# Four column strips for the conditioning products and the cached value pages of a two-layer decoder step

## What is computed

```
cmod = silu(c)                              # 1 prompt row, 8 sample rows
mod  = cmod @ ada_w[l] + ada_b[l]           # 6 x 1024 columns for each layer
hm   = rmsnorm(x, g) * (1 + sc1) + sh1      # and so on with sc2, sh2, g1, g2

p = softmax(concat([s_p, s_n]))             # sample rows: 1024 cached keys and the new one
o = einsum(p[..., :P], v_cached) + einsum(p[..., P:], v_new)
```

## Time and profile before

| | |
|---|---|
| median of three runs | 1906.09 us |
| the profiled execution | 1905.32 us, its span 1903.2 us |
| PE busy | 1763.3 us, 93% |
| DVE, ACT, POOL busy | 892.9, 597.2, 198.6 us |
| mean granted clock of TensorE | 0.954 |
| HBM | 224 MB read, 23.7 MB written |

### The profile page before, as it was taken

The page is one execution under the profiler, slowest core; times in us unless marked ns, Lnnn a source line. Parts: engine busy times, 40 slices in busy tenths (PEclk is TensorE's granted clock), DMA queues, the critical chain, the costliest instruction groups (busy, mean ns, idle before and its releaser), DMA issues.

```text
span 1903.2 us, 33709 instructions
## 1 busy us (share of the span) xinstructions
PE 1763.3 (93%) x13817; PEld 1593.5 (84%) x13817; DVE 892.9 (47%) x1470; ACT 597.2 (31%) x880; POOL 198.6 (10%) x172
## 2 busy tenths in 40 slices
PE   5899767889999999999999999999978999999997
PEld 4799744349899999998988878798748899999996
DVE  3328578764533332333625547337464533333334
ACT  2324234343432122122334334314432432122222
POOL 1006560001000000001000201101120100000001
PEclk8799777899999999999999999999988999999998
DMA  8946644556636236327232716334846133333321
GB/s 247 276 124 186 195 138 122 163 142 155 158 97 166 80 98 164 92 74 180 73 94 73 234 50 199 115 89 141 257 151 166 56 89 100 87 95 95 89 69 54
DMA packets 368714, 248.96 MB, mean 131 GB/s; under 512 B 9768, under 2 KB 338888, under 8 KB 368591
## 3 DMA queue, kind: packets, MB, share of 16 engines
q1 hardware_dynamic: 333716, 197.04, 36.8%
q0 software_dynamic: 9296, 33.82, 5.2%
q10 hardware_dynamic: 25587, 16.45, 2.9%
HBM read 224.05 MB, written 23.70 MB: 130 GB/s over the span
## 4 chain that ended last, share of the span: by engine, by line
PE 76%; DVE 11%; ACT 5%; DMA 3%; POOL 2%; issue 2%; SPq 1%; ACTq 0%; POOLq 0%; DVEq 0%
PE product L824 56%; PE product L839 4%; PE job L774 2%; DVE CV L1904 2%; POOL sqa L2364 2%; PE job L1269 2%; PE product L1017 2%; PE job L1252 1%; PE job L1186 1%; PE job L715 1%; DVE SC L1918 1%; DMA raw<-in_ada_w 1%; PE job L978 1%; DVE scaled L1831 1%; PE job L1169 1%
## 5 line engine op out<-in xcount | busy, mean ns | idle before, releaser
L824 PE MATMUL product<-H_hi,w_lo 128*128 128x260 f32 x2368 | 672.4, 284 | 5.0 <-ACT gate L1301 4.7
L824 PE MATMUL product<-H_lo,w_hi 128*128 128x260 f32 x2368 | 670.5, 283 | 0.0
L824 PE MATMUL product<-H_hi,w_hi 128*128 128x260 f32 x2368 | 670.3, 283 | 0.0
L824 PEld LDWEIGHTS product<-H_hi,w_lo 128*128 128x128 f32 x2368 | 447.8, 189 | 6.4 <-DVE w_lo L1775 5.5
L824 PEld LDWEIGHTS product<-H_lo,w_hi 128*128 128x128 f32 x2368 | 447.8, 189 | 1.4
L824 PEld LDWEIGHTS product<-H_hi,w_hi 128*128 128x128 f32 x2368 | 448.1, 189 | 0.0
L1775 DVE TENSOR_TENSOR w_lo<-raw,w_hi 128x1024 fp32r<-128x1024 f32 (+1 forms) x228 | 278.1, 1220 | 207.2 <-ACT w_hi L1301 206.5
L1301 ACT ACTIVATE w_hi<-raw 128x1024 fp32r<-128x1024 f32 (+1 forms) x228 | 234.9, 1037 | 254.9 <-PE product L824 186.8
L824 PE MATMUL product<-G_hi,w_lo 128*128 128x260 f32 x880 | 250.2, 284 | 2.7 <-DVE G_lo L1784 1.4
L824 PE MATMUL product<-G_hi,w_hi 128*128 128x260 f32 x880 | 249.4, 283 | 0.0
L824 PE MATMUL product<-G_lo,w_hi 128*128 128x260 f32 x880 | 249.3, 283 | 0.0
(11 more groups left out here) (329 smaller groups left out, 2232.5 us busy)
## 6 DMA issues: line engine op xcount, KB each, us to landing
spare<-in_ada_w SPq DMA_DIRECT2D x48, 512.0 KB, 7.3
raw<-in_w_in_odd SPq DMA_DIRECT2D x48, 512.0 KB, 3.9
raw<-in_w_ffn_gate SPq DMA_DIRECT2D x44, 512.0 KB, 4.2
raw<-in_w_ffn_up SPq DMA_DIRECT2D x44, 512.0 KB, 3.9
kp<-in_cache_k SPq DMA_DIRECT2D x64, 256.0 KB, 2.9
raw<-in_w_ffn_down SPq DMA_DIRECT2D x32, 512.0 KB, 4.6
st<-in_state_ret POOLq DMA_DIRECT2D x28, 512.0 KB, 4.7
out_ret_sample<-st POOLq DMA_DIRECT2D x28, 512.0 KB, 5.0
```

The source lines that it names most:

```text
L824: mm = pe.matmul(Gp[slot][:, c, 0:CH], w[:, j, k, :], x[:, k, cols], start=k == 0 and p == 0, stop=k == kt - 1 and p == 2)
```

## The change

The products of a contraction tile go to four strips in turn instead of two, each strip takes two of the eight tiles (or pages), and what follows handles four parts:

- conditioning products: strip by `i % 4`, the first four matmuls start their strip, the last four stop it;
- ACT copies 128 partitions instead of 64, and the `rows_` tiles are 128 partitions high;
- the turn is 128 by 128 instead of 64 rows by 128;
- DVE sums four parts with a reduce into `mod` and adds the bias in a second instruction;
- value pages: strip by `g % 4`; masking and gathering go over 104 partitions instead of 40, with the constants that they need repeated four times;
- the memset of the product banks covers 128 partitions.

The order of the work, the loads, the semaphores and the buffers are the same. The diff, without the places where a tile's height alone changes in the same way:

```diff
     at[0] = lg_at
-    vm = sb("vm", [CG + HEADS, 2, 512])
+    vm = sb("vm", [3 * CG + HEADS, 2, 512])
     at[0] = free_at
...
-    rows_early = sb("rows_early", [2 * CG, 2, 512])
+    rows_early = sb("rows_early", [P, 2, 512])
...
 
-            return slice(CG * (i % 2), CG * (i % 2) + CG)
+            return slice(CG * (i % 4), CG * (i % 4) + CG)
...
                             mm = pe.matmul(bank[group_rows(k), j * P:(j + 1) * P], cT[:, k, :], site_buffer(name)[:, b, k, :],
-                                           start=k < 2, stop=k >= KD - 2)
+                                           start=k < 4, stop=k >= KD - 4)
                     close(mm)
...
                 for j in range(4):
-                    mm = turn(bank[:, j * 2 * CG:(j + 1) * 2 * CG], ada_rows(g)[:, j * P:(j + 1) * P], 2 * CG)
+                    mm = turn(bank[:, j * P:(j + 1) * P], ada_rows(g)[:, j * P:(j + 1) * P], P)
                 close(mm)
...
-                    n.up(f(ada_rows(g), Jp[jobs.bank(("adr", g))][0:2 * CG, :], ACT.Copy), emptied["A"])
+                    n.up(f(ada_rows(g), Jp[jobs.bank(("adr", g))][:, :], ACT.Copy), emptied["A"])
...
                     pe.wait_ge(v_page[g], 16 * (b + 1))
-                    mm = pe.matmul(value_bank(b)[CG * (g % 2):CG * (g % 2) + HEADS, :], SC[:, :, b, g],
-                                   value_page(g), start=g < 2, stop=g >= 6)
+                    mm = pe.matmul(value_bank(b)[CG * (g % 4):CG * (g % 4) + HEADS, :], SC[:, :, b, g],
+                                   value_page(g), start=g < 4, stop=g >= 4)
                     mm.then_inc(v_used, 1)
...
                     mm = pe.matmul(Gp[1][:, 1, t * NB + b:t * NB + b + 1], vm[:, b % 2, t * P:(t + 1) * P],
-                                   con[0:CG + HEADS, C_PAIR:C_PAIR + 1], start=True, stop=True)
+                                   con[0:3 * CG + HEADS, C_PAIR:C_PAIR + 1], start=True, stop=True)
                 mm.then_inc(vm_used, 1)
...
             for i in range(2):
-                step(v.memset(Gp[i][0:2 * CG, :, :], 0.0))
+                step(v.memset(Gp[i][:, :, :], 0.0))
             for i in range(2):
...
 
-                turned = bank_of(("ada", g))[:, 0:8 * CG].rearrange("p (m s c) -> p m s c", s=2, c=CG)
+                turned = bank_of(("ada", g))[:, :].rearrange("p (m s c) -> p m c s", s=4, c=CG)
                 to = mod[:, 4 * g:4 * g + 4, :]
-                step(v.tensor_tensor(to, turned[:, :, 0, 0:9],
+                step(v.tensor_reduce(to, turned[:, :, 0:9, :], AX.X, ALU.add))
+                n.up(v.tensor_tensor(to, to,
                                      vec[:, V_ADAB + 4 * g:V_ADAB + 4 * g + 4].unsqueeze(2).broadcast_to((P, 4, 9)),
-                                     ALU.add))
-                n.up(v.tensor_tensor(to, to, turned[:, :, 1, 0:9], ALU.add), emptied["D"])
+                                     ALU.add), emptied["D"])
 
...
 
-            own_head = con[0:CG + HEADS, C_OWN:C_OWN + HEADS].unsqueeze(2).broadcast_to((CG + HEADS, HEADS, HD))
+            own_head = con[0:3 * CG + HEADS, C_OWN:C_OWN + HEADS].unsqueeze(2).broadcast_to((3 * CG + HEADS, HEADS, HD))
 
             def masked_values(b):
                 dve.wait_ge(v_used, 8 * b + 8)
                 if b >= 2:
                     dve.wait_ge(vm_used, b - 1)
                 n.up(v.tensor_tensor(vm[:, b % 2, :].rearrange("p (h d) -> p h d", d=HD),
-                                     value_bank(b)[0:CG + HEADS, :].rearrange("p (h d) -> p h d", d=HD),
+                                     value_bank(b)[0:3 * CG + HEADS, :].rearrange("p (h d) -> p h d", d=HD),
                                      own_head, ALU.mult), vm_ready)
...
     c[:, C_SIN:C_SIN + T] = np.sin(angle)
-    for e in (0, CG):
+    for e in range(0, P, CG):
         c[e:e + HEADS, C_OWN:C_OWN + HEADS] = np.eye(HEADS)
```

More of the change, by code:

```diff
@@ L471, in build @@
     at[0] = kt_at
-    rows_mid = sb("rows_mid", [2 * CG, 2, 512])
+    rows_mid = sb("rows_mid", [P, 2, 512])
     qs2 = sb("qs2", [P, 512], f32r)
     at[0] = vt_at
-    rows_late = sb("rows_late", [2 * CG, 2, 512])
+    rows_late = sb("rows_late", [P, 2, 512])
     CR = sb("CR", [8, T])
@@ L481, in build @@
     spare = sb("spare", [P, 8, KD, P])
-    rows_norm = sb("rows_norm", [2 * CG, 2, 512])
+    rows_norm = sb("rows_norm", [P, 2, 512])
     at[0] = us_at
@@ L520, in build @@
     at[0] = raw_at
-    rows_last = sb("rows_last", [2 * CG, 2, 512])
+    rows_last = sb("rows_last", [P, 2, 512])
     at[0] = h_at
@@ L654, in ada_rows @@
             if g >= ADA_LATE:
-                return dec[0:2 * CG, :]
+                return dec[:]
             if g < ADA_NORM:
@@ L1198, in late_step @@
                             mm = pe.matmul(Gp[b // 4][group_rows(k), 0, b % 4 * P:(b % 4 + 1) * P], cT[:, k, :],
-                                           late[:, b, k, :], start=k < 2, stop=k >= KD - 2)
+                                           late[:, b, k, :], start=k < 4, stop=k >= KD - 4)
                         mm.then_inc(late_used, 1)
@@ L1375, in take_rows @@
                     act.wait_ge(samp_dve, 1)
-                n.up(f(ada_rows(g), Gp[g % 2][0:2 * CG, 0, :], ACT.Copy), ada_taken)
+                n.up(f(ada_rows(g), Gp[g % 2][:, 0, :], ACT.Copy), ada_taken)
             def take_site_rows(name):
@@ L1700, in _ @@
                             wait_job(act, ("ada", g - 1))
-                        n.up(f(ada_rows(g), Gp[q // 4][0:2 * CG, 0, :], ACT.Copy), late_taken)
+                        n.up(f(ada_rows(g), Gp[q // 4][:, 0, :], ACT.Copy), late_taken)
                 if h == RH:
```

## The result

The changed kernel takes **1891.6 us** in the median (1886.36 to 1896.02, 6 runs), the kernel before beside it 1906.22 us (1905.74 to 1909.32, 6 runs): a ratio of 0.9918, 95% interval 0.9901 to 0.9934. Its profiled execution took 1894.45 us. The forecast of 1888.2 us was 3.4 us too low; its range of 1879 to 1904 us holds the result.

The account below looks back on a forecast made before the run. TensorE, with 76% of the chain, was taken as the bound wherever nobody else ends last. Terms of -2.2, -3.5, -10.5, +1.5, -6, +2.6 and +0.2 sum to -17.9 us, giving 1888.2 us; range 1879 to 1904 us.

Parts of the forecast that it names:

- The pace of a site: Conditioning products, 128 records per site: four strips run side by side, so 7.18 us becomes about 3.65 us.
- Rival A: Weight loads become the next limit: sites stay at 7.1 us, value pages still gain, total 1902.9 us; chance 0.09.
- Rival B: Two strips at once are the most for any product; only the additions are left, total 1908.9 us; chance 0.08.
- The first site: Ahead of the first projection pair: DVE's operand, ready at 73.55 us, becomes the limit; pair ends at 85.7 us, -2.2 us.
- The turns: Turns 128 wide instead of 64: +0.33 us at each of eight places on PE, +2.6 us.
- the feed-forward rows: Three sites in the first feed-forward, between gate/up and down blocks: 7.18 us becomes 3.65 each, -10.5 us for all.
- The sum on VectorE: DVE's sum becomes a reduce and an add: +0.1 us per group of 24, mostly hidden, +0.2 us in all.
- The norm sites: Three norm sites: PE idles some 4 us at each, the clock may fall and slow the pair behind: +1.5 us.
- The value pages: Eight attention steps of 16 records: at most 13.6 us from four strips, room 0 to -10.4, taken as -6 us.
- the two caps named: Limits on value pages: DVE's 20.3 us idle for scores in six waits; SP's page loads, with 10.4 us of room.
- Rival C: Idle PE drops the clock to 0.5 from 322 to 421 us, costing 34 us, total 1922 us; chance 0.07.
- the late stage: Late products, 1390 to 1435 us, PE busy 25.9 of 45 us: 0; -3 us if DVE did not cover it.

Follow-up runs that it names:

- e2: The changed kernel with the late products issued twice in a row: 1889.57 us, ratio 0.990 to the kernel before.
- e4: The changed kernel with value pages back in two strips, conditioning products still in four: 1894.43 us, ratio 0.9917 to the kernel before.
- e9: The changed kernel with the three norm sites and the late products back in two strips: 1889.6 us, ratio 0.9904 to the kernel before.
- e7: The changed kernel with value-page loads for samples 1 to 7 left out, sample 0's pages reused: 1891.71 us, one run.
- e8: The changed kernel with pages 4 to 7 of samples 1 to 7 issued by GpSimd, the rest by SP: 1891.2 us, ratio 0.9912.
- e6: The kernel before, two strips, with value-page loads for samples 1 to 7 left out, sample 0's pages reused: 1913.87 us, one run.
- e5: The kernel before with only the value pages in four strips, conditioning in two: 1902.94 us, ratio 0.9974 to the kernel before.

## Why the prediction was right, and where it was off

**The pace of a site: right.** "If four strips do what two do, a site takes 13.8 / 4 and a tail, about 3.65 us": 3.70. The two feed-forward sites that the table shows by themselves gave 3.43 us each from pair to pair, turn included: no other engine's work ends late behind them. Rival A, loads as the next limit, was wrong: 128 loads of 110 ns (106 to 110 ns in the changed kernel too) pass in a site of 3.70 us, so four are under way at once. Rival B has nothing left. On the weight loads, the rule of the Trainium skill (page "TensorE: Matmul & The Clock Gate", Part 3) that a load overlaps a running matmul only where the row group differs doesn't hold here: all four strips use the same rows, and with loads one after another a site would need 14.1 us for them alone. The same part gives 2.38 times for three column tiles; four strips against one would be 13.8 / 3.70 = 3.7 times, with the 13.8 worked out in the prediction.

**The first site: right, down to the operand.** The timeline of PE there, then of DVE, answers to the earlier trace rows.

```profile
64.28 1.08 PE L792 MATMUL product<-raw,cT 128*32 128x128 f32 x16 [2.01 <-DMA raw<-in_ada_w]
65.29 1.97 PE L715 MATMUL job<-con,rows_early 128*128 128x128 f32 x8
67.19 4.58 PE L774 MATMUL job<-side,cT 128*32 128x128 f32 x128
73.68 0.39 PE L839 MATMUL product<-H_hi,w_lo 128*128 128x260 f32 x1 [1.91 <-DVE H_lo L1848]
```

```profile
72.88 0.74 DVE L1848 SCALAR_TENSOR_TENSOR H_lo<-scaled,mod,H_hi 128x512 fp32r<-128x512 f32 x1
74.39 0.74 DVE L1848 SCALAR_TENSOR_TENSOR H_lo<-scaled,mod,H_hi 128x512 fp32r<-128x512 f32 x1
75.91 0.74 DVE L1848 SCALAR_TENSOR_TENSOR H_lo<-scaled,mod,H_hi 128x512 fp32r<-128x512 f32 x1
```

The pair waits 1.91 us for H_lo, which ends at 73.62 us (foreseen 73.55), DVE then delivers one every 1.51 us, and the pair ends at 85.92 (foreseen 85.7). The last raw block fell from 1.92 to 1.08 us. In three other traces (e2, e4, e9) the pair itself took 13.3 us instead of 12.24, so that the whole saving was smaller there.

**The turns: too dear.** Eight take 1.03 us for 0.71, as the forecast had it. But the wider turn starts sooner behind the last product, and its tail runs beside what follows. From the last product's start ahead of a turn to the start of the next block it was 0.85 us (603.70 to 604.55 before) and is 0.92 (592.19 to 593.11): +0.07 instead of +0.33. Ahead of the first feed-forward site it is +0.24 (0.84 and 1.08 us). At eight places that would make +0.6 to +1.9, where the forecast has +2.6. This is part of why the feed-forward rows beat the forecast.

**The sum on VectorE: right.** Its lines in the changed kernel (min/median/max ns, first and last start):

```profile
L1875 DVE TENSOR_REDUCE mod<-job x24: 243/300/308, 42.0 to 1579.7; 128x36 f32<-128x144 f32 x24
L1876 DVE TENSOR_TENSOR mod<-mod,vec x24: 195/196/932, 42.3 to 1580.0; 128x36 f32<-128x36 f32 x24
```

300 and 196 ns, where 300 was taken for the reduce; two steps of 187 ns make way, so it is 0.12 us a group, and no wait behind it shows. What was put at nothing because it keeps its columns did cost next to nothing: ACT's copy of 128 partitions takes 597 ns where that of 64 took 590, the masked multiply over 104 partitions 680 where that over 40 took 673 (medians).

**The norm sites: the mechanism right, the amount too high.** They end early and PE waits for H_lo, by the waits from 470 to 480 us:

```profile
PE product L839 <- DVE H_lo L1848: 4.1, 1, 4.1
```

before it was 0.6 us. The +1.5 was "for the norm where the pair has no wait behind it to hide in", without saying which norm that is. The slow pair came at all three, 1.0 to 2.3 us each in the first trace. And there is a wait to hide in behind the first and behind the third: PE's wait for ACT's gate is 0.7 to 0.9 us shorter there. Behind the second pair it is some 0.2 us, and that row is 0.7 us longer, turn included. So the reason given was a good one. By the table the three norms cost some +0.9 us together, turns included (-3.7 us in the first row less the 3.4 of its feed-forward site, +0.7 and +0.5), where the forecast has +2.5 with its turns.

**The value pages: the step that was mis-sized.** -6 was taken, "just over half" of the room; -4 is what the stretch gives at a like clock, -2.8 by the traces of the table and -3.8 by all. "Value pages of about 1.9 us" did not come: from first record to last a step takes 2.6 to 7.7 us in the changed kernel; 1.9 us is seen for the last three steps with the loads left out (e7), and for one with two queues (e8). The 5.95 us "at worst" was the longest piece of the chain; the last step took 7.85 us in the kernel before already, and 3.62 without loads (e6). Of the two caps named, SP's loads were there: PE now waits for pages.

```profile
DVE nm L1979 <- PE job L980: 16.9, 7, 3.6
PEld product L1017 <- DMA vp_b<-in_cache_v: 13.8, 15, 1.7
PE product L1017 <- DMA vp_b<-in_cache_v: 2.4, 5, 0.7
```

SP's wait for PE, of which "the other 10.4 are all the room that stream has", went from 36.3 us in seven waits to:

```profile
SPq L600 <- PE product L1017: 33.0, 4, 25.4
```

25.4 of it still in one, so 7.6 us are left in the other three: the chain now passes through this queue and the transfers. DVE's idle time for the scores went from 20.3 us only to 16.9. Both caps were named, each weighed alone. That they stand one behind the other, some 3 us apart, was not seen. That -6 came within some 2 us all the same is in part luck: it was a share of the room, not worked out from either chain. Rival C, the clock in this stretch, was wrong by its size (0.87 against 0.89 in the first trace, where 0.62 would have cancelled the gain). Its sign is open: from the first score on, the changed kernel's three traces are granted 0.78, 0.82 and 0.74, the two of before 0.82 and 0.85, but e4 with pages in two strips has 0.78 and e5 with four 0.85.

**The sum.** By the means of the traces the misses are +3.2 us at the value pages, +2.0 in the late stage (not shown to be the change's), and +0.4 at the end, against -1.5 in the two rows with feed-forward sites, -0.9 at the second and third norm, and some tenths: some 3 us less gained than the 17.9 forecast. So the total is close in part because misses of either sign cancel.

## What to carry to other kernels

Small fp32 matmuls of few output rows go up to four at a time when their outputs lie in four 32-partition strips, weight loads included; where nothing but TensorE ends last, the whole saving arrives. Where a stage has two more chains of nearly the same length, price each behind the other before counting a saving: here 13.5 us of products off the chain gave 4. Before filling an idle time for the sake of the clock, look for the next wait behind it, which may give back the same time. And compare several traces of one kernel before explaining a loss of a few microseconds by the change: the same instructions gave spans 7.7 us apart.

## What was not expected

- Four strips start their records within 0.04 us of each other. A record lasts 273 ns in either kernel; only the number under way changes.
- Where PE idles 3.2 to 4.1 us ahead of a norm pair (the first trace of the changed kernel), that pair is granted 0.79 to 0.87 and takes 1.0 to 2.3 us more; in the kernel before, where it idles 0.6 us at most, 1.00. In three of four traces with two strips at the feed-forward sites a low-clock stretch comes after the first norm pair instead, with PE busy (89.47 of 91.91 us in the kernel before).
- The stretches at the lower of the two clock levels, 1.2 GHz, add up to 174 and 148 us in the two traces of the kernel before and to 209, 172 and 203 in three of the changed one (mean granted clocks of 0.954, 0.961, 0.945, 0.954 and 0.946). The spans of the latter lie 7.7 us apart.
- Leaving out 56 page loads, so that the DMA share of the attention falls from 0.54 to 0.19, gained nothing in the kernel before.
